# Spare weight units moved from the last expert pair to one in the middle, and one down product put off, in a three-layer fp32 transformer kernel

## The chip, the cores and the metric

One core of a Trainium2 chip runs the whole program. The metric is the device time of one execution in microseconds (us), the median over several executions. TensorE is called PE below, VectorE DVE, ScalarE ACT, GpSimd POOL, and the queue of SyncE, which issues the weight transfers, SP.

## What is computed

512 tokens of width 1024 in fp32 go through three layers. The first has differential attention, the second a pooling mixer, the third gated attention beside a linear recurrence. Each layer ends in a mixture of 32 experts of which a token uses two:

```python
def hier_moe(t, ...):                       # layers 0 and 1; layer 2 likewise with F = 256
    # group = argmax of a group router, two experts of that group by an expert router
    y[token] = sum over its 2 experts e of  w_e * (silu(t @ gate[e]) * (t @ up[e])) @ down[e]
```

gate and up are 1024 x F, down is F x 1024, with F = 512 in mixtures 0 and 1 and F = 256 in mixture 2. So a mixture reads 32 x 3 matrices of 2 MB (F = 512) or 1 MB (F = 256), once each. The result is added to the scaled input and normalized, and goes to the next layer.

## The kernel before

**Work and loops.** `mixture(l)` exists once for each engine and walks over the experts in 16 pairs (`over_pairs`, line 315; i counts turns of two pairs, q the pair in the turn, s the expert in the turn). Pair 0, 1 and 12 to 15 are written out, 2 to 11 are a hardware loop. A pair has up to 64 tokens of each of its two experts.

**PE in a pair** (line 1107): gate and up products of the first expert, then of the second (`gate_up`, line 1066); half of the rows of the next pair are gathered (`ahead`, line 970 with one-hot selection matrices, or line 1018 where mixture 2 has them gathered by DMA); the products silu(gate)*up are transposed (`turn_products`, line 1088); the other half of `ahead`; then the two down products (`down`, line 1101). In the last pair there is no next pair: `turn_last_selection` (line 1025) stands in its place, ahead of `turn_products`. ACT takes the silu of the gates (line 1385) and copies the down results out of PSUM (lines 1396, 1397), DVE multiplies (line 1844) and copies the transposed product (line 1962). POOL stores each pair's rows to `y_rows` in HBM by an indirect DMA (line 2235).

**Weights.** SP loads them in the order in which PE uses them into a ring of 12 units of 1 MB each. A matrix of 2 MB takes two units and is one transfer, unless it begins in unit 11: then it is two transfers of 1 MB (`load_matrix`, line 558). A load waits until PE has used what lay in its units 12 units earlier (`units_used`); PE counts a unit as used at the end of an expert's gates and ups, and after each half of a down matrix. A pair is 12 units with F = 512 and 6 with F = 256.

**Spares.** Places that are free in a mixture (h, hT, gaps in the work area) hold units outside the ring: 5 units in mixtures 0 and 1 (the gate and half of the up matrix of one expert, the gate of the other), 4 in mixture 2 (all gates and ups of a pair). `load_spares` issues them behind pair 0's loads, `load_scraps` (mixture 2) behind pair 1's. They belong to the last pair, experts 30 and 31, which so needs 7 (or 2) units of the ring. `gate_up_units` (line 335) and `down_unit` (line 349) give the place of each matrix in the ring's order.

**The end of a mixture.** ACT writes the scaled residual into h in the last pair (`residual`, line 1399; h is a spare until then). POOL stores pair 14, reads the number of overflow blocks and raises `over_moved` (line 2266); SP then loads tiles 0 and 1 of `y_rows` (`load_tiles`, line 631), which waits for the store of pair 14 and, in mixtures 0 and 1, for the residual. The rows of the last pair are added by PE in PSUM (`sum_last_pair`, line 672) and by DVE (`combine_tile` line 1531, `add_last` line 1557, `combine_with_last` line 1545). In mixture 2 POOL fetches the gain of the last norm (line 2244) after the store of pair 14, ahead of `over_moved`, and SP asks for all four tiles.

## Time and profile before

| | |
|---|---|
| median of 3 executions | 2067.46 us (2064.28 to 2069.76) |
| the profiled execution | 2057.91 us |
| its span, first to last instruction | 2056.1 us |
| PE / DVE / ACT / POOL busy | 1919.0 / 672.8 / 403.2 / 152.6 us |
| granted PE clock, mean | 0.983 |
| bytes moved | 598.95 MB, mean 291 GB/s |
| mixture 0, from pair 0's first product | 338.7 to 813.4 us |
| mixture 1 | 983.2 to 1455.3 us |
| mixture 2 | 1785.4 to 2032.2 us |

The profiled execution was 9.6 us shorter than the median of the three timed ones. Busy shares are averages over stages with different limits; the chain of waits, followed back from the last instruction, tells for each stretch whether PE or the weight stream set the time.

### The profile page before, as it was taken

How to read it: one execution, taken by the hardware profiler on the slowest of the kernel's cores; microseconds unless marked ns; L12 is line 12 of the kernel's file. 1: busy time of each engine (PE TensorE's matmuls, PEld its weight loads, DVE VectorE, ACT ScalarE, POOL GpSimd, SP SyncE). 2: the span in 40 equal slices, each digit the busy share in tenths (PEclk: the TensorE clock that was granted, in tenths of full speed). 3: DMA queues.
4: the chain of work that ended last, by engine and by line, in shares of the span. 5: the costliest groups of instructions: out<-in, count | busy, mean ns of one | idle time of the engine just before them, and what ended most of it. 6: DMA issues, size and time to landing. Idle time of an engine off the chain costs nothing.

```text
span 2056.1 us, 24625 instructions
## 1 busy us (share of the span) xinstructions
PE 1919.0 (93%) x9773; PEld 1036.8 (50%) x9773; DVE 672.8 (33%) x1622; ACT 403.2 (20%) x866; POOL 152.6 (7%) x208
## 2 busy tenths in 40 slices
PE   8989999999999998999999999999799999998787
PEld 4444456455545543746545545545554445765443
DVE  0156665311111112636221111111739323632114
ACT  1134431111111013110111011011324322121122
POOL 0111101000000000000100000000010001211100
PEclk9999999999999999999999999999999999999999
DMA  9711108999999996723999999998841211799995
GB/s 336 218 47 48 45 24 306 426 427 428 427 428 428 427 425 242 273 78 138 366 426 428 427 428 428 427 426 362 297 134 47 77 41 35 281 383 419 420 418 212
DMA packets 100353, 598.95 MB, mean 291 GB/s; under 512 B 14553, under 2 KB 43113, under 8 KB 61743
## 3 DMA queue, kind: packets, MB, share of 16 engines
q1 hardware_dynamic: 84639, 568.05, 68.6%
q0 software_dynamic: 15632, 29.79, 4.3%
q8 instruction: 54, 0.88, 0.2%
q14 instruction: 28, 0.23, 0.0%
HBM read 575.58 MB, written 37.03 MB: 298 GB/s over the span
## 4 chain that ended last, share of the span: by engine, by line
PE 60%; DMA 28%; DVE 7%; ACT 2%; issue 2%; SPq 1%; POOL 0%; DVEq 0%; ACTq 0%
DMA ring<-in_moe_w_up_dram 21%; PE bank L1066 19%; PE bank L713 9%; DMA ring<-in_w_up_dram 6%; PE bank L1101 6%; PE bank L866 5%; PE bank L970 5%; PE bank L727 3%; PE bank L699 3%; PE bank L1240 2%; PE bank L1201 1%; PE bank L815 1%; PE bank L1217 1%; PE bank L746 1%; DMA work<-work 1%
## 5 line engine op out<-in xcount | busy, mean ns | idle before, releaser
L1066 PE MATMUL bank<-ring,work 128*64 128x512 f32 (+1 forms) x2928 | 562.0, 532 | 53.8 <-DMA ring<-in_moe_w_up_dram 31.0
L1066 PEld LDWEIGHTS bank<-ring,work 128*64 128x64 f32 x2928 | 232.7, 140 | 370.8 <-issue 342.5
L1844 DVE TENSOR_TENSOR work<-work,bank 64x512 f32<-64x512 f32 (+1 forms) x96 | 86.4, 900 | 794.2 <-ACT work L1385 794.2
L1101 PE MATMUL bank<-ring,work 128*64 128x512 f32 x1280 | 286.9, 599 | 6.2 <-DVE work L1962 6.2
L970 PEld LDWEIGHTS bank<-work 128*128 128x128 f32 x2048 | 233.6, 192 | 25.2 <-issue 25.1
L970 PE MATMUL bank<-work 128*128 128x128 f32 x2048 | 242.7, 277 | 0.0
L713 PE MATMUL bank<-hT,ring 128*128 128x512 f32 x512 | 234.4, 599 | 0.7 <-ACT work L1303 0.7
L1101 PEld LDWEIGHTS bank<-ring,work 128*64 128x64 f32 x1280 | 90.0, 137 | 168.6 <-issue 160.7
L1385 ACT ACTIVATE work<-bank 64x512 f32<-64x512 f32 (+1 forms) x96 | 50.0, 521 | 526.1 <-PE bank L1066 525.1
L1396 ACT ACTIVATE work<-bank 64x512 f32<-64x512 f32 x96 | 56.7, 590 | 482.7 <-PE bank L1101 482.7
L713 PEld LDWEIGHTS bank<-hT,ring 128*128 128x128 f32 x512 | 92.8, 192 | 103.9 <-issue 101.9
L2235 POOL DMA_INDIRECT y_rows<-work,y_row x47 | 45.9, 977 | 984.5 <-ACT work L1397 871.4
L1836 DVE COPY work<-bank 128x512 f32<-128x512 f32 x93 | 64.3, 691 | 161.1 <-PE bank L970 154.8
L727 PE MATMUL bank<-ring,hT 128*128 128x512 f32 x192 | 83.3, 593 | 0.5 <-DMA ring<-in_attn_w_qkv_dram 0.5
L699 PE MATMUL bank<-hT,ring 128*128 128x128 f32 x512 | 61.3, 282 | 1.3 <-ACT hT L1279 1.2
L699 PEld LDWEIGHTS bank<-hT,ring 128*128 128x128 f32 x512 | 59.8, 197 | 3.2 <-ACT hT L1279 3.2
L727 PEld LDWEIGHTS bank<-ring,hT 128*128 128x128 f32 x192 | 36.2, 190 | 45.7 <-issue 44.0
L866 PE MATMUL bank<-ring,hT 128*128 128x512 f32 x128 | 57.8, 596 | 1.0 <-ACT hT L1279 1.0
L1397 ACT ACTIVATE work<-bank 64x512 f32<-64x512 f32 x96 | 57.0, 594 | 1.1
L866 PE MATMUL bank<-ring,work 128*128 128x512 f32 x128 | 56.2, 594 | 0.8 <-ACT work L1443 0.8
L1279 ACT ACTIVATE hT<-bank 128x512 f32<-128x512 f32 x56 | 31.1, 596 | 128.6 <-PE bank L746 128.5
L2179 POOL DMA_DIRECT2D work<-work x64 | 32.1, 508 | 187.9 <-ACT work L1351 187.9
(313 smaller groups left out, 1619.6 us busy)
## 6 DMA issues: line engine op xcount, KB each, us to landing
ring<-in_moe_w_down_dram SPq DMA_DIRECT2D x63, 2048.0 KB, 17.0
ring<-in_moe_w_up_dram SPq DMA_DIRECT2D x62, 2048.0 KB, 20.2
ring<-in_moe_w_gate_dram SPq DMA_DIRECT2D x60, 2048.0 KB, 16.5
ring<-in_w_down_dram SPq DMA_DIRECT2D x32, 1024.0 KB, 25.9
ring<-in_w_gate_dram SPq DMA_DIRECT2D x30, 1024.0 KB, 21.0
ring<-in_w_up_dram SPq DMA_DIRECT2D x30, 1024.0 KB, 23.0
ring<-in_attn_w_qkv_dram SPq DMA_DIRECT2D x12, 1024.0 KB, 14.2
work<-y_rows SPq DMA_DIRECT2D x12, 1024.0 KB, 7.0
```

The costliest lines, as they stand in the source:

```text
L699: mm = pe.matmul(bank[2 * i + half][:, P * tt:P * tt + P], v[:, k, P * half:P * half + P], hT[:, k, P * tt:P * tt + P], start=(k == 0), st ...
L713: mm = pe.matmul(banks[:, :], v[:, k, 128 * half:128 * half + 128], hT[:, k, :], start=(k == 0), stop=(k == K - 1))
L727: mm = pe.matmul(banks[tt][:, :], operand[:, 4 * kk + k, P * tt:P * tt + P], v[:, k, :], start=(kk + k == 0), stop=(kk + k == 4))
L866: mm = pe.matmul(bk[:, :], operand(k, tt), v[:, k % 4, :], start=(k == (0 if l else 4)), stop=(k == last))
L970: mm = pe.matmul(XT[half][:, P * k:P * k + width], src[:, tt, c0:c0 + P], sel[buf][:, tt, 0:width], start=(tt == 0), stop=(tt == T - 1))
L1066: mm = pe.matmul(GU2[of_pair][(gate_rows, up_rows)[a][of_pair], 0:F], xgT[pair % 2][:, per * kk + k, BLK * of_pair:BLK * of_pair + BLK], v ...
L1101: mm = pe.matmul(DN2[par][BLK * n:BLK * n + BLK, :], hT_[:, 2 * kk + k, BLK * par:BLK * par + BLK], v[:, k, 512 * n:512 * n + 512], start= ...
L1385: act.activation(sg_pair[own_rows[par], 0:F], GU2[par][gate_rows[par], 0:F], ACT.Silu)\
L1396: act.activation(y[own_rows[par], 0:512], DN2[par][0:BLK, :], ACT.Copy)
L1397: act.activation(y[own_rows[par], 512:D], DN2[par][BLK:P, :], ACT.Copy).then_inc(main.ysb, 1)
L1836: dve.tensor_copy(xgT[buf][:, 4 * half:4 * half + 4, 0:width], XT[half][:, :].rearrange("p (k n) -> p k n", k=4)[:, :, 0:width])\
L1844: dve.tensor_tensor(dealt(hg_pair[own_rows[par], 0:F], F // P), as_dealt(sg_pair[own_rows[par], 0:F], F // P), as_dealt(GU2[par][up_rows[p ...
```

## The change

The spares go to another pair, `SPARE_PAIR`: pair 4 in mixtures 0 and 1, pair 5 in mixture 2. From the pair behind it on every place in the ring's order is 5 (or 4) units lower, and the last pair takes all its 12 (or 6) units from the ring. In mixtures 0 and 1 the places change between even and odd, so that from there on one matrix of a pair begins in unit 11 and is loaded in two transfers. The residual moves to the pair behind the spare one. Pairs 0 to 5 are written out and 6 to 11 are the loop.

The down product of expert 29 (`put_off`), and its load, stand in the last pair behind all its gates and ups and ahead of the transposition of its products; its result is copied out, and pair 14 stored, accordingly later. `turn_last_selection` goes behind `turn_products`. The gain of the last norm is fetched one pair earlier.

```diff
+SPARE_PAIR = (4, 4, 5)
@@ over_pairs
-            for q in range(2):
-                pair(0, q)
-            with eng.Fori(1, E // TURN - 2) as i:
+            for i in range(3):
+                for q in range(2):
+                    pair(i, q)
+            with eng.Fori(3, E // TURN - 2) as i:
@@
+        def put_off(i, s):
+            return type(i) is int and TURN * i + s == E - 3
+
+        def downs(i, q):
+            own = [s for s in (2 * q, 2 * q + 1) if not put_off(i, s)]
+            return [2 * q - 1] + own if last_pair(i, q) else own
+
+        def spare_pair(m, i, q):
+            return nth_pair(i, q) == SPARE_PAIR[m.l]
+
+        def first_unit(m, i, q):
+            before = nth_pair(i, q) is not None and nth_pair(i, q) <= SPARE_PAIR[m.l]
+            return 2 * m.upb * q - (0 if before else SPARES[m.l])
+
         def gate_up_units(m, i, s):
-            first_unit, halves = 2 * m.upb * (s // 2), m.ng // 2
-            if last_pair(i, s // 2):
+            u, halves = first_unit(m, i, s // 2) - (m.nd if last_pair(i, s // 2) else 0), m.ng // 2
+            if spare_pair(m, i, s // 2):
                 if m.l == 2:
                     return {}
-                return {(1, 0): first_unit + 1, (1, 1): first_unit + 2} if s % 2 else {(1, 1): first_unit}
+                return {(1, 0): u + 1, (1, 1): u + 2} if s % 2 else {(1, 1): u}
@@ down_unit
-            return 2 * m.upb * (s // 2) + 2 * m.ng + m.nd * (s % 2) - (SPARES[m.l] if last_pair(i, s // 2) else 0)
+            if put_off(i, s):
+                return first_unit(m, i, s // 2 + 1) - m.nd + 2 * m.ng
+            spared = SPARES[m.l] if spare_pair(m, i, s // 2) else 0
+            return first_unit(m, i, s // 2) + 2 * m.ng + m.nd * (s % 2) - spared
@@ load_spares, load_scraps: the same with E - 1
-                    sp.dma_start(spare_gate[0], matrices(l, E - 2)[0]).then_inc(spare_loaded, 16)
+                    sp.dma_start(spare_gate[0], matrices(l, 2 * SPARE_PAIR[l])[0]).then_inc(spare_loaded, 16)
@@ SP, pair
-                    for s in (2 * q, 2 * q + 1):
+                    for s in downs(i, q):
@@ PE, gate_up
-                    if last_pair(i, pair) and of_pair == 0:
+                    if spare_pair(m, i, pair) and of_pair == 0:
                         pe.wait_ge(spare_loaded, spare_count[l])
@@ PE, pair
                     gate_up(i, 2 * q)
                     gate_up(i, 2 * q + 1)
+                    late, own = (downs(i, q)[:1], downs(i, q)[1:]) if last_pair(i, q) else ([], downs(i, q))
+                    for s in late:
+                        down(i, s)
+                    if not last_pair(i, q):
+                        ahead(i, q, 0)
+                    turn_products(i, q)
                     if last_pair(i, q):
                         turn_last_selection()
-                    else:
-                        ahead(i, q, 0)
-                    turn_products(i, q)
@@
-                    down(i, 2 * q)
-                    down(i, 2 * q + 1)
+                    for s in own:
+                        down(i, s)
@@ ACT, pair: also around residual(2), residual(3)
-                    if last_pair(i, q) and l < 2:
+                    if nth_pair(i, q) == SPARE_PAIR[l] + 1 and l < 2:
                         residual(0)
                         residual(1)
@@
-                    result(i, 2 * q)
-                    result(i, 2 * q + 1)
+                    for s in downs(i, q):
+                        result(i, s)
@@ POOL, mixture
-                    if l == 2 and q == E // 2 - 2:
+                    if l == 2 and q == E // 2 - 3:
                         pool.wait_ge(spare_used, 1)
                         bcast(lnp[:, D:2 * D], t["final_norm_2"].unsqueeze(0), par.rms, D)
```

## Rows read from the trace of the kernel before

**Rows 1.** The page: the chain that ended last, by line.
```profile
DMA ring<-in_moe_w_up_dram 21%; PE bank L1066 19%; PE bank L713 9%; DMA ring<-in_w_up_dram 6%; PE bank L1101 6%; PE bank L866 5%; PE bank L970 5%; PE bank L727 3%; PE bank L699 3%; PE bank L1240 2%; PE bank L1201 1%; PE bank L815 1%; PE bank L1217 1%; PE bank L746 1%; DMA work<-work 1%
```

**Rows 2.** Chain of waits, mixture 0's first pairs: start us, us, what.
```profile
338.74 13.95 PE bank L1066 x64
...
424.89 13.76 PE bank L1066 x64
...
439.45 21.00 DMA ring<-in_moe_w_up_dram
```

**Rows 3.** Chain of waits, mixture 0's pairs 14 and 15.
```profile
740.26 23.97 DMA ring<-in_moe_w_up_dram
...
764.37 8.43 PE bank L1066 x32
...
780.58 7.02 PE bank L1101 x32
...
803.11 0.67 PE bank L1088 x4
...
803.80 0.70 DVE work L1962
...
804.55 8.81 PE bank L1101 x32
...
816.76 0.70 DVE h L1557
```

**Rows 4.** Windows: us; PE, PEld, DVE, ACT, POOL busy; PEclk, DMA share, GB/s.
```profile
340.00:350.00 10.00, 10.00 (x50) 3.33 (x48) 1.63 (x3) 2.10 (x3) 2.54 (x3) 1.00 0.61 208
480.00:785.00 305.00, 288.70 (x1642) 148.16 (x1640) 47.20 (x77) 35.46 (x61) 9.73 (x10) 0.99 1.01 427
785.00:790.00 5.00, 5.00 (x26) 1.58 (x22) 0.00 (x0) 1.59 (x3) 0.39 (x1) 1.00 0.38 161
```

**Rows 5.** Chain of waits, mixture 1's pairs 14 and 15.
```profile
1409.40 7.09 PE bank L1066 x32
...
1448.23 7.11 PE bank L1101 x32
```

**Rows 6.** Chain of waits, mixture 2: pair 6, then pairs 14 and 15.
```profile
1877.34 3.69 PE bank L1066 x32
...
2010.03 3.69 PE bank L1066 x32
...
2028.49 3.68 PE bank L1101 x16
```

**Rows 7.** DMA issues, us to landing: one from 345.8 us, one from 490.1 us.
```profile
ring<-in_moe_w_gate_dram SPq DMA_DIRECT2D x1, 2048.0 KB, 8.2
...
ring<-in_moe_w_up_dram SPq DMA_DIRECT2D x1, 2048.0 KB, 21.0
```

**Rows 8.** Instructions in order of time, ACT, POOL, SP and DVE, 2014 to 2048.
```profile
2020.16 0.59 ACT L1397 ACTIVATE work<-bank 64x512 f32<-64x512 f32 x1
...
2021.53 0.97 POOL L2235 DMA_INDIRECT y_rows<-work,y_row  x1 [14.91 <-ACT work L1397]
2023.29 0.60 POOL L2160 DMA_DIRECT2D work<-in_final_norm_dram  x1 [0.79 <-PE bank L1066]
...
2026.63 2.09 SPq L639 DMA_DIRECT2D work<-y_rows  x4
...
2034.01 2.60 DVE L1531 SCALAR_TENSOR_TENSOR h<-work,h 128x1024 f32<-128x1024 f32 x2 [4.98 <-DMA work<-y_rows]
2036.65 1.41 DVE L1557 TENSOR_TENSOR h<-h,bank 128x512 f32<-128x512 f32 x2
2039.02 1.53 DVE L1545 SCALAR_TENSOR_TENSOR h<-work,bank 128x512 f32<-128x512 f32 x2 [0.97 <-PE bank L680]
```

**Rows 9.** DMA issues, us to landing: the first tile in mixture 0.
```profile
work<-y_rows SPq DMA_DIRECT2D x1, 1024.0 KB, 4.9
```

**Rows 10.** Groups of instructions: busy us, mean ns of one, idle before.
```profile
L1401 ACT ACTIVATE h<-work 128x1024 f32<-128x1024 f32 x8 | 15.5, 1996 | 0.0
```

More of the change, by code:

```diff
@@ L333, in last_pair @@
             return nth_pair(i, q) == E // 2 - 1
+        def put_off(i, s):
[8 more added lines that the diff above has]
+            return 2 * m.upb * q - (0 if before else SPARES[m.l])
         def gate_up_units(m, i, s):
-            first_unit, halves = 2 * m.upb * (s // 2), m.ng // 2
-            if last_pair(i, s // 2):
+            u, halves = first_unit(m, i, s // 2) - (m.nd if last_pair(i, s // 2) else 0), m.ng // 2
+            if spare_pair(m, i, s // 2):
                 if m.l == 2:
                     return {}
-                return {(1, 0): first_unit + 1, (1, 1): first_unit + 2} if s % 2 else {(1, 1): first_unit}
-            return {(a, kk): first_unit + m.ng * (s % 2) + halves * a + kk for a in range(2) for kk in range(halves)}
+                return {(1, 0): u + 1, (1, 1): u + 2} if s % 2 else {(1, 1): u}
+            return {(a, kk): u + m.ng * (s % 2) + halves * a + kk for a in range(2) for kk in range(halves)}
         def gu_used(m, i, s):
@@ L420, in program @@
                   con[:, C_CAUS:C_CAUS + 256], sm(128, 256)]
-        last_gates = [spare[0].rearrange("p a n -> p (a n)").rearrange("p (k n) -> p k n", k=K)[:, k, :] for k in range(K)]
-        last_ups = [spare[1].rearrange("p a n -> p (a n)").rearrange("p (k n) -> p k n", k=K)[:, k, :] for k in range(K)]
+        spare_gates = [spare[0].rearrange("p a n -> p (a n)").rearrange("p (k n) -> p k n", k=K)[:, k, :] for k in range(K)]
+        spare_ups = [spare[1].rearrange("p a n -> p (a n)").rearrange("p (k n) -> p k n", k=K)[:, k, :] for k in range(K)]
         spare_up = lnp.rearrange("p (k n) -> p k n", k=K)
@@ L531, in load_spares @@
                     sp.wait_ge(tiles_written, turns[HEADS[l][1]].src_all)
-                    sp.dma_start(spare_gate[0], matrices(l, E - 2)[0]).then_inc(spare_loaded, 16)
+                    sp.dma_start(spare_gate[0], matrices(l, 2 * SPARE_PAIR[l])[0]).then_inc(spare_loaded, 16)
                     sp.wait_ge(routing.logits, T * (l + 1))
                     for n in range(2):
-                        sp.dma_start(gaps[n], matrices(l, E - 2)[1][:, D * n:D * n + D]).then_inc(spare_loaded, 16)
-                    sp.dma_start(spare_gate[1], matrices(l, E - 1)[0]).then_inc(spare_loaded, 16)
+                        sp.dma_start(gaps[n], matrices(l, 2 * SPARE_PAIR[l])[1][:, D * n:D * n + D]).then_inc(spare_loaded, 16)
+                    sp.dma_start(spare_gate[1], matrices(l, 2 * SPARE_PAIR[l] + 1)[0]).then_inc(spare_loaded, 16)
                 def load_scraps():
@@ L541, in load_scraps @@
                     for a in range(2):
-                        sp.dma_start(spare[a].rearrange("p a n -> p (a n)"), matrices(l, E - 1)[a])\
+                        sp.dma_start(spare[a].rearrange("p a n -> p (a n)"), matrices(l, 2 * SPARE_PAIR[l] + 1)[a])\
                             .then_inc(spare_loaded, 16)
-                    gate, up, _ = matrices(l, E - 2)
+                    gate, up, _ = matrices(l, 2 * SPARE_PAIR[l])
                     sp.wait_ge(tiles_written, turns[HEADS[l][1]].src_all)
@@ L1054, in rows_of @@
                             if of_pair:
-                                return (last_gates, last_ups)[a]
+                                return (spare_gates, spare_ups)[a]
                             return [spare_up[:, k, :] for k in range(K)] if a else scraps
@@ L1410, in pair @@
                     product(i, 2 * q + 1)
-                    if last_pair(i, q) and l < 2:
+                    if nth_pair(i, q) == SPARE_PAIR[l] + 1 and l < 2:
                         residual(2)
                         residual(3)
-                    result(i, 2 * q)
-                    result(i, 2 * q + 1)
+                    for s in downs(i, q):
+                        result(i, s)
                 over_pairs(act, pair)
```

## The prediction

> **What bounds the kernel now.** I read the page first. PE is busy for 93% of the span (1919.0 of 2056.1 us), but the chain that ended last lies for 21 + 6 = 27% of it in ring transfers of the mixtures [rows 1]. So PE's busy share hides a second limit. The chain in order of time shows which holds where.
>
> In mixture 0, pairs 0 to 2 take PE (424.89 - 338.74)/3 = 28.72 us each without a wait; then a transfer ends each stretch. The last up of pair 4 lands at 439.45 + 21.00 = 460.45, that of pair 14 at 740.26 + 23.97 = 764.23 [rows 2, 3], so the stream needs 303.8/10 = 30.38 us for a pair of 12 units with its row store, 2.53 us a unit. It is never idle from 480 to 785 and then stops: share 0.38 in the next 5 us [rows 4]. PE is not done by then. From its product on pair 14's last up, at 764.37, to the end of the mixture at 804.55 + 8.81 = 813.36 it works for 49.0 us on what the ring already holds [rows 3]. **That is the place**: a late stretch set by PE while the DMA rests, after 300 us set by the DMA while PE waited. Mixture 1 is alike: 1409.40 to 1448.23 + 7.11 = 1455.34, 45.9 us [rows 5]. In mixture 2 pairs 6 to 14 take (2010.03 - 1877.34)/8 = 16.6 us, 2.76 us a unit, and PE ends at 2028.49 + 3.68 = 2032.17 [rows 6].
>
> **Spares in the middle, mixtures 0 and 1.** The stream's length stays 187 units, so the last unit can't come much earlier. What changes is what is left for PE behind it. The last needed up is now that of pair 15, with three down matrices (6 units) behind it in the order; pair 14's had 11 units behind it. So it comes 5 units later than pair 14's did: 5 x 2.53 = 12.7 us.
>
> To this comes what the stream loses where the ring is full. Pair 4 starts at 424.89 + 28.72 = 453.6 and now uses 7 units. All loads up to pair 5's last up are then landed 7 units behind 460.45: 460.45 + 17.7 = 478.2. The next, pair 5's first down matrix, may go when pair 4's first down is done. Between the products and the downs lie 28.72 - 13.76 - 7.02 = 7.94 us, so that is 453.6 + 13.76 + 7.94 + 3.51 = 478.8. A 2 MB load into a nearly empty queue took 8.2 us to land [rows 7] and so lands at 487.0, where a full queue would have had it at 478.2 + 5.1 = 483.3. I take the **loss as 3.8 us**, once; the next load that must wait goes at the end of pair 5's first gates and ups, 489.5, 2.5 us ahead of the queue's end. Bounds: 0, if the transfers still under way when a landing is told bridge the gap, and 7.6, if it runs dry twice. The Trainium skill ("DMA: Bandwidth & Descriptors", section "Anatomy of one DMA — SWDGE (gpsimd) path") has about 2 us plus the bytes at 436 GB/s for one DMA, 6.8 us for 2 MB. By it the loss would be 2.4 us, and the whole sum 2.8 us better; the row decides.
>
> **The down put off.** Behind the last up's landing PE has: gates and ups 7.1 (7.09 in mixture 1 [rows 5]), expert 29's down 3.51, transposes 0.67, then the hT copy 0.76 with the last selection's transposes beside it, two downs 7.02 [rows 3]: 19.1 us. The 3.51 us fills what is a stall today, while ACT and DVE make the last product. I let the clock stay full; 8.43 for 7.1 is the bound, as pair 14 showed [rows 3]. The down matrices land 5 us apart, ahead of their use.
>
> So the stretch is 12.7 + 3.8 + 19.1 = 35.6 us: mixture 0 gains 49.0 - 35.6 = **13.4**, mixture 1 gains 45.9 - 35.6 = **10.3**. PE alone would end mixture 0 at 453.6 + 11 x 28.72 + 13.76 + 0.67 + 0.76 + 7.02 = 791.7 (one pair's gather less), ahead of 764.4 + 35.6 = 800.0, so the stream still sets it. Its lead on PE, 12.7 - 3.8 = 8.9 us, shrinks by 30.38 - 28.72 = 1.66 us a pair: no waits in pairs 5 to 9, then waits again.
>
> **What the end of mixtures 0 and 1 gives back.** Pair 14's rows are now copied out 8.5 us before the end instead of a pair before it. ACT takes 2 x 0.59 us; in mixture 2 POOL started 0.8 us behind ACT, its store took 0.97, and SP asked 2.7 us behind POOL's last DMA, the gain's fetch (2023.89 to 2026.63) [rows 8]. The same steps stand here. So SP asks at the end - 2.8, tile 0 is there 4.9 us later [rows 9], DVE adds it in 2.60 us: end + 4.7. Today DVE goes on at 816.76, end + 3.4 [rows 3]. **Loss 1.3 us** in each, bounds 0 and 2.7. The later tiles are needed over 10 us behind the end, so their 2 us of delay are covered, as are the next layer's first loads.
>
> **Mixture 2.** Pair 15's up comes one unit later than pair 14's: 2010.03 + 2.76 = 2012.8. Then 3.69, one down at 1.84, 0.95 for half as many transposes and a smaller copy than mixture 0's 0.67 + 0.76, and 3.68: PE ends at 2023.0, 9.2 us earlier. But the tiles set the end there: DVE stood idle for them until 2034.01, and PE had been done [rows 8]. Expert 29's down ends at 2018.3, the store starts at 2020.3 instead of 2021.53 and the fetch of the gain, 1.4 us with its wait, is out of the way: SP asks at 2024.0 instead of 2026.63. The first tile took 2034.01 - 2026.63 = 7.4 us behind that fetch, 4.9 in mixture 0 [rows 8, 9]; I take 4.9, the nearer case now. DVE then has tile 0 done at 2024.0 + 4.9 + 2.60 + 1.41 = 2032.9 instead of 2039.02: **gain 6.1**, with 7.4 it is 3.6. The stream there runs no risk of a full ring: 4 units of lead in a ring that holds two pairs.
>
> **At nothing:** the residual (four copies of 2.0 us on ACT, two and two, in pair 5 [rows 10]) lies under 6.9 us of PE products and 7.9 us of gathers; without that cover it would hold up pair 5 once, by 4 us. The two half transfers per pair cost SP one more issue, under loads queued 21 us ahead [rows 7]. The spares are landed long before pair 4: the DMA ran empty in 340 to 350 [rows 4]. More code written out: pairs 12 to 15 are so today under a full stream and show no other wait.
>
> **Sum:** 13.4 + 10.3 + 6.1 - 2 x 1.3 = 27.2 us. The profiled execution, 2057.91, would be 2030.7; it was 9.6 us under the median of 2067.46, against which I forecast **2040.3 us**.
>
> **Rivals.**
> - *The stream loses nothing* and the tiles cover their delay: 2 x (3.8 + 1.3) = 10.2 us more, 2030.1. For it: the share of 1.01 through every earlier wait. Chance 0.22.
> - *The ends take more back*: the queue runs dry twice in each (7.6 more), and each end loses 2.7 (2.8 more): 2050.7. With the slow clock and the late tile too, 2.6 + 2.5, 2055.8. For it: every step of the ask is on the path now. Chance 0.21.
> - *The change moves the lead but doesn't use it*: the ring can't hold the 5 units' lead, the stream rests 12.7 us in pairs 4 and 5 and ends that much later. Then 2 x 8.9 = 17.8 us and mixture 2's 6.1 fall away: 2064.2. Against it: at 453.6 about 21 us of loads are under way, more than 12.7 [rows 7]. Chance 0.04.
> - *Slower: the ring's edge.* Behind the spare pair the places are odd, a matrix straddles the edge, and SP holds everything behind its half. If the queue ran dry once in every pair from 5 on, at 8.2 - 5.1 = 3.1 us each, 11 of them would cost 34.1 in place of 3.8, in both mixtures 60.6 us more: 2100.9. It turns slower from 27.2/(2 x 3.1), 4 to 5 more dry spells in each mixture. Against it: loads lay 21.0 us in the queue, four matrices. Chance 0.03.
>
> **How the numbers follow.** The forecast has 0.50. The range from the best to the worst sum, 2028 to 2056, takes in the first two rivals and 2 us of spread of the medians. A measurement can tell about 0.3% (6.2 us) from no change; the first three cases, forecast included, are faster by more: 0.93. The fourth is the same: 0.04. Slower: 0.03.
>
> **What would show it.** Right: no PE wait for a ring transfer in pairs 5 to 9 of mixtures 0 and 1, small ones from 10 on; a dip of the DMA near 479; pair 15's last up landing near 780.5, mixture 0 ending 35 to 36 us behind pair 14's old landing, at 800; DVE waiting for tile 0 at each end; mixture 2's SP request before the down products' end plus 2 us. Wrong: a DMA share under 0.9 over more than 5 us in the middle, a wait on `spare_loaded`, or a half unit ending a PE wait in every pair.

## The result and the profile after

| | before | after |
|---|---|---|
| median of 4 executions each | 2068.61 us (2064.28 to 2070.09) | 2040.17 us (2039.23 to 2048.76) |
| ratio | | 0.9875, 95% interval 0.9844 to 0.9906 |
| the profiled execution / its span | 2057.91 / 2056.1 us | 2040.23 / 2038.4 us |
| PE busy | 1919.0 us | 1915.2 us |

The medians differ by 28.4 us; the ratio, with which the interval goes, says 1.25%, 26 us. The change is faster. The forecast was 2040.3 us and 27.2 us of gain.

The two profiled executions differ by only 17.7 us, and that must be cleared up before they are compared. In the changed one, mixture 0 starts at 348.25, in the other at 338.74 [rows 2]. That is 9.5 us in a part that the change does not touch; over the thirteen profiles of this study this start lay between 338.7 and 348.8. So I cut every profiled execution into stages that begin and end with a product of PE. "mixture" is its first gate product to the end of its last down product, "between" from there to the next mixture's first product, "end" from mixture 2's last down product to the end of the span, "waits" what PE stood idle for ring transfers in mixtures 0 and 1.

| us | to mixture 0 | mixture 0 (waits) | between | mixture 1 (waits) | between | mixture 2 | end |
|---|---|---|---|---|---|---|---|
| before | 338.7 | 474.6 (16.6) | 169.9 | 472.1 (14.4) | 330.0 | 246.8 | 24.0 |
| after | 348.2 | 460.6 (6.7) | 172.5 | 463.5 (9.8) | 328.0 | 239.4 | 26.1 |

The mixtures give 14.0 + 8.6 + 7.4 = 30.0 us. The stretch behind each takes some back: the next layer's projection starts 12.9 us behind mixture 0's last down instead of 10.7, 19.0 behind mixture 1's instead of 17.4, and the end is 2.1 longer: 5.9 us. That makes **24.1 us**. The other 3.1 us, with which span and start would give 27.2, lie in untouched work between the mixtures, nearly all between 1 and 2, where the profiles scatter too (327.6 to 333.4).

The page's chain by line. The transfers of the ring were 21 + 6% [rows 1] and are 12 + 5%:

```profile
PE bank L1091 22%; DMA ring<-in_moe_w_up_dram 12%; PE bank L738 9%; PE bank L1126 8%; PE bank L995 8%; PE bank L891 5%; DMA ring<-in_w_up_dram 5%; PE bank L724 3%; PE bank L752 3%; PE bank L1268 1%; PE bank L1229 1%; PE bank L840 1%; DMA work<-work 1%; PE bank L1245 1%; PE bank L771 1%
```

The chain of waits in mixture 0 of the changed kernel (start us, us, what). L1091 are gates and ups (L1066 before), L1126 downs (L1101), L1424 ACT's first copy of a down result, L1585 the first tile's sum with the last pair's rows, L724 the next layer:

```profile
463.24 13.73 PE bank L1091 x64
...
577.36 13.76 PE bank L1091 x64
...
591.85 21.07 DMA ring<-in_moe_w_up_dram
...
711.08 23.28 DMA ring<-in_moe_w_up_dram
...
734.50 8.78 PE bank L1091 x32
...
758.08 13.73 PE bank L1091 x64
...
779.59 3.58 PE bank L1126 x16
783.17 13.83 PE bank L1091 x64
797.00 3.45 PE bank L1126 x16
...
800.47 0.59 ACT work L1424
...
802.44 3.89 DMA y_rows<-work,y_row
...
806.39 5.01 DMA work<-y_rows
...
814.07 0.70 DVE h L1585
...
821.92 8.01 PE bank L724 x64
```

Read it against [rows 2, 3]. Pair 4, which has the spares now, starts at 463.24, and pairs 4 to 8 follow each other without a wait. The first wait is in pair 9, begun 28.5 us behind pair 8, at 605.9: its last up lands at 591.85 + 21.07 = 612.92. The last is in pair 13. **Pairs 14 and 15 don't wait at all**: their 64 gate and up products run in one piece (13.73 and 13.83). Behind the last up that it needed from the stream PE had 49.0 us of work before; now this is pair 15's last up, and from its product (783.17 + 6.87 = 790.04) to the end are 808.90 - 790.04 = 18.9 us. The trace has no landing for that up; the second down matrix behind it landed at 799.58, and at 4.9 us a matrix (the landing of the last one, 804.47, less 799.58) I estimate 789.8 for the up. So PE waits for nothing from 734.50 on, but at the end the stream is only some 0.3 us ahead of it.

PE at the end of mixtures 0 and 2, in order of time (start us, us, engine, line, operation, tiles; in brackets the idle time before):

```profile
800.37 0.66 PE L1113 MATMUL bank<-con,work 128*128 128x128 f32 x4
800.86 0.60 PE L1050 MATMUL bank<-con,work 128*128 128x128 f32 x4
801.81 7.09 PE L1126 MATMUL bank<-ring,work 128*64 128x512 f32 x32 [0.35 <-DVE work L1990]
...
2008.67 3.65 PE L1126 MATMUL bank<-ring,work 128*64 128x512 f32 x16
```

The turned selection (L1050) lies ahead of the copy for which PE waits anyway; 0.35 us of idle time are left before the last downs.

The windows show what the forecast called the dip (us; PE, PEld, DVE, ACT, POOL busy; granted PE clock, DMA share, GB/s). It was put near 479 and lies at 485 to 490, which is 9.5 us later, like everything:

```profile
480.00:485.00 5.00, 5.00 (x45) 4.76 (x45) 1.50 (x3) 0.00 (x0) 0.00 (x0) 1.00 1.00 426
485.00:490.00 5.00, 5.00 (x26) 1.70 (x24) 0.48 (x1) 1.18 (x2) 0.00 (x0) 1.00 0.48 144
490.00:495.00 5.00, 5.00 (x26) 1.61 (x24) 0.00 (x0) 1.18 (x2) 0.97 (x1) 1.00 0.91 383
600.00:700.00 100.00, 97.02 (x544) 47.98 (x542) 13.98 (x21) 13.00 (x22) 3.88 (x4) 1.00 1.01 427
```

Against 427 GB/s the two middle windows lack (427 - 144)/427 x 5 = 3.3 and 0.5 us, their two neighbours behind some tenths: the stream **ran dry for about 4.3 us**, 4.2 in mixture 1. In all other 5 us windows of the middle it is full.

The end of mixture 2: the chain, then DVE in order of time:

```profile
2002.39 3.67 PE bank L1091 x32
...
2009.78 2.65 DMA y_rows<-work,y_row
...
2012.50 4.70 DMA work<-y_rows
```

```profile
2017.23 2.60 DVE L1559 SCALAR_TENSOR_TENSOR h<-work,h 128x1024 f32<-128x1024 f32 x2 [7.91 <-DMA work<-y_rows]
```

SP asks 0.2 us behind PE's last down (2008.67 + 3.65 = 2012.32), DVE stands idle for 7.91 us, and the chain goes through the store and the first tile: the tiles set the end now. In the kernel before they did not. DVE was idle for them too, 4.98 us [rows 8], but waited once more behind them, 0.97 us for PE's sum of the last pair [rows 8], and the chain of before goes through that sum:

```profile
2038.06 0.87 PE bank L680 x2
...
2039.02 0.76 DVE h L1545
```

e1 and e10 below agree: their first tile is there 3.7 us earlier, counted from PE's last down, and their end is as long as before (23.9 in both, 24.0 before).

### The profile page after: what moved, and what is told of

Read it like the earlier page. It is cut to its first block, busy times and chain, and to the rows that moved or that the text cites. A ratio compares the mean times of both kernels' runs of the same rounds, so it can differ in the third digit from the quotient of the medians.

```text
span 2038.4 us, 24272 instructions
## 1 busy us (share of the span) xinstructions
PE 1915.2 (94%) x9773; PEld 1032.6 (51%) x9773; DVE 673.2 (33%) x1622; ACT 402.3 (20%) x866; POOL 152.3 (7%) x208
## 4 chain that ended last, share of the span: by engine, by line
PE 68%; DMA 20%; DVE 7%; ACT 2%; issue 2%; SPq 0%; POOL 0%; another core or an unknown queue 0%; DVEq 0%; POOLq 0%
PE bank L1091 22%; DMA ring<-in_moe_w_up_dram 12%; PE bank L738 9%; PE bank L1126 8%; PE bank L995 8%; PE bank L891 5%; DMA ring<-in_w_up_dram 5%; PE bank L724 3%; PE bank L752 3%; PE bank L1268 1%; PE bank L1229 1%; PE bank L840 1%; DMA work<-work 1%; PE bank L1245 1%; PE bank L771 1%
## 5 line engine op out<-in xcount | busy, mean ns | idle before, releaser
L1091 PE MATMUL bank<-ring,work 128*64 128x512 f32 (+1 forms) x2928 | 555.8, 528 | 36.3 <-DMA ring<-in_w_up_dram 18.8
L1091 PEld LDWEIGHTS bank<-ring,work 128*64 128x64 f32 x2928 | 227.3, 138 | 352.8 <-issue 326.2
L1126 PE MATMUL bank<-ring,work 128*64 128x512 f32 x1280 | 285.8, 596 | 4.2 <-DVE work L1990 4.1
L1126 PEld LDWEIGHTS bank<-ring,work 128*64 128x64 f32 x1280 | 89.2, 137 | 165.2 <-issue 156.9
L1424 ACT ACTIVATE work<-bank 64x512 f32<-64x512 f32 x96 | 56.6, 589 | 475.4 <-PE bank L1126 475.4
L724 PE MATMUL bank<-hT,ring 128*128 128x128 f32 x512 | 60.6, 280 | 1.5 <-ACT hT L1307 1.5
L724 PEld LDWEIGHTS bank<-hT,ring 128*128 128x128 f32 x512 | 59.1, 195 | 3.4 <-ACT hT L1307 3.4
L1307 ACT ACTIVATE hT<-bank 128x512 f32<-128x512 f32 x56 | 30.9, 595 | 127.7 <-PE bank L771 127.7
## 6 DMA issues: line engine op xcount, KB each, us to landing
ring<-in_moe_w_up_dram SPq DMA_DIRECT2D x61, 2048.0 KB, 16.6
```

What stands on the lines that cost most here:

```text
L724: mm = pe.matmul(bank[2 * i + half][:, P * tt:P * tt + P], v[:, k, P * half:P * half + P], hT[:, k, P * tt:P * tt + P], start=(k == 0), st ...
L1091: mm = pe.matmul(GU2[of_pair][(gate_rows, up_rows)[a][of_pair], 0:F], xgT[pair % 2][:, per * kk + k, BLK * of_pair:BLK * of_pair + BLK], v ...
L1126: mm = pe.matmul(DN2[par][BLK * n:BLK * n + BLK, :], hT_[:, 2 * kk + k, BLK * par:BLK * par + BLK], v[:, k, 512 * n:512 * n + 512], start= ...
L1424: act.activation(y[own_rows[par], 0:512], DN2[par][0:BLK, :], ACT.Copy)
```

## The experiments

Eleven runs were made in three groups, each group on a chip of its own with the kernel before beside it: e1 to e4 (before: 2065.06 us), e5 to e8 (2060.25) and e9 to e11 (2063.27). Each had 5 or 6 executions, e2 twelve. None leaves work out. A median compares only within its group. Stages as above, in us, from one profiled execution each; "behind 0" and "behind 1" are the start of the next projection behind the mixture's last down.

| | median | ratio to before, 95% | mixture 0 | behind 0 | mixture 1 | behind 1 | mixture 2 | end |
|---|---|---|---|---|---|---|---|---|
| before | | | 474.6 | 10.7 | 472.1 | 17.4 | 246.8 | 24.0 |
| after | 2040.17 | 0.9875, 0.9844 to 0.9906 | 460.6 | 12.9 | 463.5 | 19.0 | 239.4 | 26.1 |
| changed again (e11) | 2041.07 | 0.9892, 0.9875 to 0.9908 | 460.9 | 12.7 | 461.7 | 18.6 | 238.4 | 26.2 |
| e1 spares only | 2046.25 | 0.9914, 0.9896 to 0.9931 | 464.5 | 10.7 | 465.4 | 17.4 | 240.8 | 23.9 |
| e2 down put off only | 2067.29 | 1.0006, 0.9990 to 1.0021 | 470.2 | 12.9 | 472.1 | 21.2 | 245.5 | 26.7 |
| e3 gain fetched late | 2043.36 | 0.9893, 0.9875 to 0.9911 | 460.8 | 12.5 | 463.8 | 18.7 | 237.4 | 27.6 |
| e4 spares at pair 2 | 2050.96 | 0.9930, 0.9911 to 0.9950 | 465.2 | 12.3 | 469.1 | 18.9 | 238.4 | 26.1 |
| e5 spares at pair 6 | 2032.23 | 0.9874, 0.9850 to 0.9898 | 461.0 | 12.0 | 459.7 | 18.8 | 239.6 | 26.2 |
| e6 eight pairs written out | 2039.89 | 0.9908, 0.9886 to 0.9930 | 461.5 | 12.4 | 461.6 | 18.7 | 237.8 | 26.2 |
| e7 four spares | 2036.57 | 0.9883, 0.9860 to 0.9905 | 460.3 | 14.3 | 464.7 | 19.0 | 238.2 | 26.2 |
| e8 spares at pair 12 | 2040.35 | 0.9903, 0.9880 to 0.9926 | 466.4 | 11.9 | 465.8 | 18.9 | 238.0 | 26.6 |
| e9 spares in two pairs | 2038.48 | 0.9880, 0.9863 to 0.9898 | 458.8 | 12.7 | 459.8 | 19.0 | 238.6 | 27.6 |
| e10 as e9, no put-off in 2 | 2040.82 | 0.9890, 0.9871 to 0.9909 | 461.9 | 12.5 | 459.1 | 19.8 | 241.4 | 23.9 |

The stages leave out the untouched stretches, which scatter by 10 us, but they scatter too. Profiles of the same order of work differ by 3.1 us in mixture 0 (e9, e10), by 2.2 in mixture 1 (after, e3, e6, e11) and by 2.2 in mixture 2 (237.4 to 239.6 in the nine with the changed order). What is smaller than that is not shown by one profile, and where the executions say something else than the stages, it is said.

### e1, e2: each part alone

```diff
 # e1: nothing is put off (the places in the ring follow, here and in e2)
-            return type(i) is int and TURN * i + s == E - 3
+            return False
-            return [2 * q - 1] + own if last_pair(i, q) else own
+            return own
 # e2: the spares stay in the last pair, the residual with them; six pairs written out, gain fetched early
-SPARE_PAIR = (4, 4, 5)
+SPARE_PAIR = (15, 15, 15)
```

> The spares sit in the middle, expert 29's down stays in pair 14. Theory (the stream sets the end, and the put-off gives only what lies behind the last landing): pair 15's last up lands 2 units (5.1 us) later, behind it PE has 17.3 instead of 19.1 us, so each of mixtures 0 and 1 is 3.3 us longer than in the changed kernel (460.7 and 463.6 us from first product to last down), and the end of a mixture gets back the 1.3 to 2.7 us that the late store of pair 14 costs. Mixture 2 is 1 to 2 us longer and its end shorter by as much. In all 0 to 4 us above the changed kernel: 2040 to 2044 us. Rival (the put-off down is what gains, because it fills the stall behind the last products in all three mixtures and keeps the clock up): 10 us or more above the changed kernel.

> The spares stay in the last pair, only the down is put off (and the last norm's gain is fetched before the store of pair 14). Theory: PE's late stretch behind pair 14's last up shrinks by the stall of some 3 us in mixtures 0 and 1, the end of each gives 1.3 to 2.7 us back, so 0 to 4 us under the kernel before. Rival (the put-off carries the gain): 10 to 20 us under the kernel before.

With the spares alone the mixtures are 10.1 + 6.7 + 6.0 = 22.8 us shorter than before, and nothing comes back behind them (10.7, 17.4, 23.9). Its six executions say less: 0.86%, 17.8 us, interval 14 to 21; the profiled one was the fastest of them, 7.6 us under their median, which at 2046.25 lies above the 2040 to 2044 expected. The chain of e1 shows why the ends stay as they were: pair 14's rows are stored in time, SP asks 13.5 us ahead of mixture 0's end (804.95), and DVE goes on from PE's products alone.

```profile
764.55 22.88 DMA ring<-in_moe_w_up_dram
...
787.57 7.10 PE bank L1091 x32
...
797.84 7.11 PE bank L1126 x32
...
808.35 0.70 DVE h L1585
```

SP's queue in e1, in order of time:

```profile
791.42 1.49 SPq L664 DMA_DIRECT2D work<-y_rows  x2
```

Against e1, putting the down off shortens the mixtures by 3.9, 1.9 and 1.4 us, 7.2 together, and lengthens what is behind them by 2.2, 1.6 and 2.2, 6.0 together: 1.2 us of gain. With e11 in place of the first profile it is 9.7 and 5.5, 4.2 us, and e3, which differs from the changed kernel by the gain's fetch alone, has a median 2.9 us under e1's. All of this is inside the scatter. Alone (e2) the put-off is no gain: where 0 to 4 us were expected, the ratio is 1.0006 and the stages give 5.7 us in the mixtures and lose 8.7 behind them. So **the spares carry the change**; the put-off down is worth 1 to 4 us there, less than can be told. It fills one stall and opens another: pair 14's rows, needed by all that follows, come a pair later. e1 also has the residual and the last selection moved, the early fetch and six pairs written out; e3 and e6 test the last two, the first two were not run apart.

### e3: the gain fetched where it was

```diff
-                    if l == 2 and q == E // 2 - 3:
+                    if l == 2 and q == E // 2 - 2:
```

> The changed kernel with the last norm's gain fetched behind the store of pair 14 again. Theory: SP asks for the tiles of mixture 2 about 1.4 us later and the first tile lands up to 2.5 us later behind the fetch's traffic: 1.4 to 3.9 us above the changed kernel, all of it behind mixture 2's last down. Rival (the request hangs on the store's landing, not on POOL's next steps): under 0.5 us.

The end is 27.6 us, 1.5 longer. SP asks at 2009.70, 0.2 us behind PE's last down as in the changed kernel, so the fetch doesn't hold up the request; that hangs on the landing of pair 14's store. The first tile is there 6.2 us behind the request in place of 4.7: in this trace the late fetch costs only as a neighbour of the tiles. The ratio can't show it, and the end scatters by as much: e9 fetches early and has 27.6 too, since its store took 3.87 us to land and not 2.65.

### e4, e5, e6, e8: where the spares go

```diff
-SPARE_PAIR = (4, 4, 5)
+SPARE_PAIR = (2, 2, 5)     # e5: (6, 6, 5); e8: (12, 12, 5), with twelve pairs written out
@@ e5, and e6 with the old SPARE_PAIR: two more pairs written out
-            for i in range(3):
+            for i in range(4):
-            with eng.Fori(3, E // TURN - 2) as i:
+            with eng.Fori(4, E // TURN - 2) as i:
```

> Spares of mixtures 0 and 1 at pair 2 instead of 4. Theory (the ring is full when the spare pair comes, and the stream runs dry for the time that it was ahead): at pair 2 the stream is about 3.3 us further ahead of PE, so its dry time is 7.1 instead of 3.8 us and each of mixtures 0 and 1 is 3.3 us longer, 464 and 467 us; 6.6 us in all, 2047 us. Rival (the ring's odd places, not the full ring, make the stream dry): no change in mixtures 0 and 1 beyond 1 us.

> Spares of mixtures 0 and 1 at pair 6, eight pairs written out and four in the loop. Theory: by pair 6 the stream is no longer ahead, so the spare pair leaves no dry time in it (no window under 0.9 there), and PE is late for 3.7 us in pairs 4 and 5 instead; the end comes 3 us earlier in each of mixtures 0 and 1 than in the changed kernel (458 and 460 us, where the clock stays full at the end), 4 to 7 us in all: 2034 to 2036 us. Rival (PE's work from the first wait on already sets the end, so nothing is left in the stream): 0 to 2 us, since PE's start of pair 6 is later by as much as the stream gains.

> The changed kernel with eight pairs written out instead of six, nothing else moved: the control for the run with the spares at pair 6. Theory: instructions come in time, no difference within 1 us in any mixture. Rival (written-out code has to be fetched through a full DMA queue): each mixture longer by some us, with PE idle for no transfer.

> Spares of mixtures 0 and 1 at pair 12, twelve pairs written out. Theory: PE waits for the stream up to pair 11 as in the kernel before, and from pair 12 on its own work sets the end: 3.9 us later than in the changed kernel in each of mixtures 0 and 1, 8 us in all, 2048 us. Rival (the place does not matter as long as it is not the last pair, since the stream's length sets the end): within 1 us of the changed kernel.

**e4** is the test of the full ring. Two pairs earlier, the stream leads PE by 3.3 us more (two pairs of 30.38 - 28.72), and the surplus must be lost. The windows of e4 (columns as above):

```profile
420.00:425.00 5.00, 5.00 (x44) 4.72 (x43) 1.90 (x3) 0.59 (x1) 0.00 (x0) 1.00 0.93 338
425.00:430.00 5.00, 5.00 (x39) 3.71 (x39) 1.14 (x2) 0.00 (x0) 0.00 (x0) 1.00 0.40 167
430.00:435.00 5.00, 5.00 (x26) 1.60 (x24) 0.00 (x0) 1.19 (x2) 0.00 (x0) 1.00 0.45 134
```

The three windows of e4 lack 7.5 us together, 3.2 more than in the changed kernel, and mixture 0 is 4.6, mixture 1 5.6 us longer. The executions agree: the median is 7.6 us over e3's, where 6.6 in all were expected. A stream rest in the middle is paid at the end; that the stages lost 1.4 and 2.4 us more than the 3.2 is about their scatter.

**e5** was to have no dry time at pair 6, and has 3.2 us of it. Its windows:

```profile
535.00:540.00 5.00, 5.00 (x39) 3.90 (x40) 1.47 (x3) 0.00 (x0) 0.00 (x0) 1.00 0.95 400
540.00:545.00 5.00, 5.00 (x26) 1.70 (x24) 0.00 (x0) 1.19 (x2) 0.00 (x0) 1.00 0.55 177
```

I had taken the lead that the stream still has at pair 4 for its cause, but at pair 6 that lead is about nothing. What remains is the step of five units at once, and I work it out so: the spare pair uses 7 units of the ring, and these land within 7 x 2.53 = 17.7 us, while PE frees the next place only 6.9 + 7.9 + 3.5 = 18.3 us behind its middle, and that load is a lone one and needs 7.6 us to land (issued at 488.38 in the changed kernel), where a full queue lands a matrix every 5.1: 18.3 + 7.6 - 17.7 - 5.1 = 3.1 us of dry time. e7 and e9, which take smaller steps, bear it out; e8 shows that it isn't all.

The mixtures of e5 are 0.5 and 1.9 us shorter than those of its control e6, which is within the scatter. Its executions are better than that: the median is 7.7 us under e6's, four of its six lie under the fastest of e6. That is what was expected (2034 to 2036), by a mechanism that the trace denies, and the two profiles don't show where it comes from. So pair 6 may be the better place; why stays open.

**e6**: no mixture is more than 0.9 us longer than in the changed kernel: more code written out costs nothing that can be seen, as forecast.

**e8**: at pair 12 the spares come when PE has waited for the stream in the pairs before, and from pair 12 on PE sets the end alone. The chain of e8, pairs 11 to 15:

```profile
652.16 24.52 DMA ring<-in_moe_w_up_dram
...
676.81 8.58 PE bank L1088 x32
...
700.19 13.73 PE bank L1088 x64
...
728.72 13.73 PE bank L1088 x64
...
782.35 13.73 PE bank L1088 x64
```

Four pairs without a wait: the lead that the spares give is not used up when the mixture ends. Mixtures 0 and 1 are 4.9 and 4.2 us longer than e6's, where 3.9 stood: 2.9 and 2.6 us more of waits, part of the rest at the slow clock (mixture 0 has two products of 8.78 and 8.58 us, e6's one). But the executions don't bear it out: medians of 2040.35 and 2039.89 us, where 8 us more were expected. The stream runs dry here too, and for longer:

```profile
720.00:725.00 5.00, 5.00 (x32) 2.71 (x32) 0.69 (x1) 0.00 (x0) 0.00 (x0) 1.00 0.21 88
725.00:730.00 5.00, 5.00 (x26) 1.72 (x24) 0.00 (x0) 2.37 (x4) 0.00 (x0) 1.00 0.79 279
```

These lack 4.0 + 1.7 us, at a place where the stream has no lead at all and five units alone would make it 3.1. A slow product just before it (8.58 for 7.1 us) makes PE free its places 1.5 us later and would be part of it; no run settles the rest. So an early place (pair 2) loses by stages and executions, the last pair by both, and between pairs 4, 6 and 12 the stages and the executions don't give one order.

### e7: one spare unit less

```diff
-SPARES = (5, 5, 4)
+SPARES = (4, 4, 4)
@@ gate_up_units: both halves of expert 8's up come through the ring
-                return {(1, 0): u + 1, (1, 1): u + 2} if s % 2 else {(1, 1): u}
+                return {(1, 0): u + 2, (1, 1): u + 3} if s % 2 else {(1, 0): u, (1, 1): u + 1}
```

> Four spare units instead of five in mixtures 0 and 1: in mixture 0 all places stay even, so that no matrix straddles the ring's edge; in mixture 1 every place is odd from pair 0 on. Theory (a unit outside the ring is worth one unit's time, and the edge costs nothing): both mixtures 0 and 1 are 2.5 us longer than in the changed kernel, less up to 1 us of dry time, 3 to 5 us in all: 2043 to 2045 us. Rival (the straddling matrix costs): mixture 0 as fast as before or faster than in the changed kernel, mixture 1 slower by well over 2.5 us.

I had counted 2.5 us a unit. Mixture 0 is 0.3 us shorter, mixture 1 1.2 longer, and the median lies 3.3 us under e6's, so the unit is not missed. The window at the dip says what went against it; the dip is nearly gone:

```profile
485.00:490.00 5.00, 5.00 (x26) 1.62 (x24) 0.00 (x0) 2.37 (x4) 0.00 (x0) 1.00 0.87 315
```

That lacks 1.3 us. Summed over the same 35 us around the dip, e7 lacks 2.0 us in mixture 0 and 2.4 in mixture 1, the changed kernel by this count 4.2 and 4.4. **The fifth spare of one pair should buy 2.5 us and costs 2.1 of dry time.** Mixture 0 has no split transfer here; in mixture 1, which begins at an odd place, nearly every pair has a split up matrix (28 transfers of 1 MB of up matrices against none in mixture 0). Against e6 on the same chip mixture 0 is 1.2 us shorter and mixture 1 3.1 us longer. That is the sign that a cost of the splits would have, at the edge of the scatter, so e7 doesn't settle whether they are free.

### e9, e10, e11: the five spares in two pairs

```diff
+SECOND = 6
@@ eight pairs written out as in e6; first_unit and down_unit follow the two steps
@@ gate_up_units: pair 4 takes gate 8 and half of up 8 from spares, pair 6 the gate of expert 13
-                return {(1, 0): u + 1, (1, 1): u + 2} if s % 2 else {(1, 1): u}
+                return {(0, 0): u + 1, (0, 1): u + 2, (1, 0): u + 3, (1, 1): u + 4} if s % 2 else {(1, 1): u}
+            if nth_pair(i, s // 2) == SECOND and m.l < 2 and s % 2:
+                return {(1, 0): u + 4, (1, 1): u + 5}
@@ load_spares
-                    sp.dma_start(spare_gate[1], matrices(l, 2 * SPARE_PAIR[l] + 1)[0]).then_inc(spare_loaded, 16)
+                    sp.dma_start(spare_gate[1], matrices(l, 2 * SECOND + 1)[0]).then_inc(spare_loaded, 16)
 # e10, beside this: no put-off in mixture 2
-            return type(i) is int and TURN * i + s == E - 3
+            return l < 2 and type(i) is int and TURN * i + s == E - 3
```

> In mixtures 0 and 1 three of the five spare units are used in pair 4 and two in pair 6, instead of all five in pair 4; eight pairs are written out instead of six, as in the control e6; mixture 2 is as changed. Theory of the full ring: with all five in pair 4 the stream ran dry for 4.3 us (mixture 0) and 4.2 us (mixture 1). With three of them the free room of the ring is never far enough behind for the queue to empty, and the two of pair 6 come when PE's lead is small again. So no 5 us window in the middle has a DMA share under 0.9, the stream ends 3.7 to 4.3 us earlier in each mixture, mixture 0 takes 457, mixture 1 459 to 460, and the whole is 7 to 8 us under the changed kernel on the same chip: about 0.9835 to 0.985 of the kernel before. Rival, the late products set the end and not the dry spell: mixtures 0 and 1 gain 2 us together at most, the ratio is that of the changed kernel within 0.001. Against the theory speaks the run with four spares, where 3.0 us less dry time paid only for the unit given away.

> As e9, and in mixture 2 the 30th expert's down stands where it stood before the change. From the run with the spares alone, the put-off was worth 1.4 us in mixture 2 and cost 2.2 us at its end: so mixture 2 takes 240.8 and the end 23.9, together 0.8 us less than e9, which is under what five rounds can tell; only the stages can show it. Rival: the put-off in mixture 2 pays (the end stays at 26 although nothing is put off): 1.4 us more than e9.

> The changed kernel once more, as the comparison on the same chip for the two above: mixture 0 460.6 and mixture 1 463.5, each within 1.7 us (one product at the slow clock), ends 12.9, 19.0 and 26.1, ratio to the kernel before 0.9875 to 0.991.

In e9 the dry spell is gone. The windows behind pair 4's and pair 6's use of the spares:

```profile
480.00:490.00 10.00, 10.00 (x55) 4.15 (x55) 0.69 (x1) 2.37 (x4) 0.00 (x0) 1.00 1.00 423
...
540.00:545.00 5.00, 5.00 (x26) 1.72 (x24) 0.00 (x0) 1.19 (x2) 0.00 (x0) 1.00 0.95 380
```

But mixtures 0 and 1 are only 2.1 and 1.9 us shorter than in e11, about half of what was expected, and in e10, the same work there, 1.0 longer and 2.6 shorter. The medians on the same chip are 2038.48 and 2041.07 us, 2.6 us apart where 7 to 8 were expected; e10's is 2040.82. e11 itself came out as expected but for mixture 1, 1.8 us shorter. The chain in mixture 0 shows for this pair of profiles where the other half is. e9, pairs 13 and 14:

```profile
728.66 7.10 PE bank L1098 x32
...
736.22 23.17 DMA ring<-in_moe_w_up_dram
...
759.52 7.09 PE bank L1098 x32
```

e11, pairs 13 and 14:

```profile
708.86 23.63 DMA ring<-in_moe_w_up_dram
...
732.62 8.65 PE bank L1091 x32
...
756.07 13.73 PE bank L1091 x64
```

Mixture 0 began at 344.8 in e9, at 345.9 in e11. PE begins pair 13's last half 728.66 - 344.8 = 383.9 us behind the start in e9, 732.62 - 345.9 = 386.7 in e11: the stream is 2.8 us earlier. In e11 this was the last wait and PE sets the rest; in e9 the stream still sets pair 14, 759.52 - 728.66 = 30.9 us on, where PE alone takes 28.5. That gives 2.3 us back, and of the rest 1.55 us is only the clock (8.65 against 7.10 us): 2.8 - 2.3 + 1.55 = 2.1. So the dry spell is real, and what its removal brings the stream is lost again where PE is the limit; in this pair of profiles 0.5 us is left beside the clock. Of all versions only e5 lies clearly under its control, in its executions and not in its stages.

In mixture 2, e10 is 2.8 us longer than e9 (241.4 against 238.6) and its end 3.7 shorter (23.9 against 27.6). The difference, 0.9 us, is what was expected, but 1.4 of the 3.7 are the late store of e9; against the changed kernel's 26.2 (e11) e10 gets 2.3. The medians (2040.82 against 2038.48) go the other way. What e10 shows is that the end goes back to its old length when nothing is put off.

## Why the prediction was right

The time came out at 2040.17 where 2040.3 stood, closer than the forecast's terms deserve. One by one:

| step | forecast | measured |
|---|---|---|
| mixture 0 shorter | 13.4 | 14.0 |
| mixture 1 shorter | 10.3 | 8.6 |
| mixture 2, PE's end earlier | 9.2 | 7.4 |
| behind mixtures 0 and 1, longer | 1.3 and 1.3 | 2.2 and 1.6 |
| behind mixture 2, longer | 9.2 - 6.1 = 3.1 | 2.1 |
| sum | 27.2 | 24.1 |

- **The place was right.** What bounded mixtures 0 and 1 was a late stretch of 49 us that PE worked alone behind 300 us in which it waited. e1 shows that moving the spares alone gives 22.8 us by its stages and 17.8 by its executions, and e2 that without it there is no gain.
- **The dry time of the stream was right in size and place**: 4.3 and 4.2 us for 3.8 (bounds 0 and 7.6). e4 makes it longer and pays for it, e7 and e9 make it shorter. With the landing time of the trace, 8.2 us [rows 7], the forecast had 3.8; the Trainium skill ("DMA: Bandwidth & Descriptors", section "Anatomy of one DMA — SWDGE (gpsimd) path"), whose fit is for DMAs that GpSimd issues while SyncE issues these, gave an estimate of 2.4. The lone load took 7.6 us here, between the two (6.8 and 8.2) and a little nearer to the row of the trace.
- **The waits came back in pair 9**, one pair earlier than forecast, and by 0.3 us only: the lead was 12.7 - 4.3 = 8.4 us and not 8.9, and shrinks by 1.85 a pair and not by 1.66, since PE takes (577.36 - 463.24)/4 = 28.53 us for a pair here. 8.4 - 5 x 1.85 is below nothing.
- **Mixture 0: 14.0 for 13.4.** The stretch from the spare pair's start to the end came as forecast: 799.4 in the old count (808.90 - 9.51) for 800.0. The forecast had the stream set the end, and small waits up to it; in the trace the last wait is in pair 13, and then PE and the stream reach that last up together, the stream an estimated 0.3 us ahead. That mixture 0 gains more than mixture 1 is in the forecast only because two products at the end of the one trace of before ran at the slow clock there (8.43 and 8.81 us for 7.1 [rows 3]), 3.1 us, and none in mixture 1 [rows 5]. The stall ahead of the second of them is in e1 too, and there it took 7.11. So 3.1 of the 13.4 us were the luck of one profile, and the changed kernel's mixture 0 has a slow product of its own (8.78).
- **Mixture 1: 8.6 for 10.3, a term that was mis-sized.** "I let the clock stay full" was the step. After its last wait, in pair 14, the product ran for 8.78 us and not 7.1 (8.43 stood beside it as the bound); that is 1.7 us, the whole gap. From there on PE set the end here, not the stream. The same happened in mixture 0, in pair 13, and is in its 14.0. The chain in mixture 1:

```profile
1399.16 8.78 PE bank L1091 x32
```

- **Mixture 2: 7.4 for 9.2.** Behind the last up PE took 9.9 us (2002.39 to 2012.32), forecast 10.2: right. The last up itself came 229.5 us behind the mixture's start (1772.9); pair 14's had come 224.6 behind it, and one unit of 2.76 was allowed for where it took 4.9. Why the stream lost 2.1 us there no run settles; the other eight profiles with this order have 237.4 to 239.6 in the stage, 238.3 in the mean, so half of it is scatter.
- **The ends: 2.2, 1.6 and 2.1.** The mis-sized step in mixtures 0 and 1 is that "SP asks at the end - 2.8, tile 0 is there 4.9 us later". SP asks 2.5 us ahead of mixture 0's end and the tile is there 5.0 us later, so that DVE comes to the last pair's rows at 814.07, 5.2 us behind the end and not 4.7; 0.4 us more come in behind it. SP's request hangs on the landing of the store, 3.89, 2.83 and 2.65 us on the chain, which the forecast took as a distance from POOL's last DMA. The value stayed inside its bounds (0 and 2.7). In mixture 2 the forecast said that "the tiles set the end there" before the change; they did not, PE's sum did, and putting the down off is what brought the tiles onto the path, for 2.1 us. The number held since the forecast compared with 2039.02, which stands behind PE's sum.
- **The gain fetched early**: of its two terms the one on the tile's landing shows in e3 (4.7 us against 6.2, where 4.9 and 7.4 stood), the one on the request, "1.4 us with its wait, is out of the way", does not: SP asks at the same moment in both.
- Of the rivals, "the lead moved but not used" falls with e1 and the chain. "Slower, the ring's edge" falls with the windows of the changed kernel, where no dry spell repeats in the pairs behind (427 GB/s from 600 to 700); a small cost of the edge is not excluded (e7). "The stream loses nothing" falls with the windows. "The ends take more back" was partly true: the ends of mixtures 0 and 1 lost 1.2 us more than forecast, of the 2.8 that it had for them, and the slow clock came in once in each of these mixtures, 1.7 us each.

That the sum of 27.2 and the median agree within 0.2 us is luck: the stages give 24.1, and the interval of the ratio holds 19 to 32 us. The changed kernel run again gave 22.3 (1.08% of 2063.27, interval 19 to 26). Both intervals hold the stages' 24.1.

## What to carry to other kernels

Look in the chain for the last wait of a stage, and then at what the other engine still has to do behind it: prefetched work in store is worth more in the middle, where the stream sets the time, than at the end, where it doesn't. Release it in steps no larger than what the consumer frees while the stream refills, or the ring runs full and the queue empties: here the fifth unit at once bought nothing that could be measured. Before an operation is put off to fill a stall, follow its result: the put-off down saved 7.2 us on PE and cost 6.0 in the tiles behind it. An engine that stands idle for a transfer is not yet bound by it: see what it waits for next. And set the profile of one execution beside the times of the others; twice here they disagreed by more than the effect looked for.

## What was not expected of the hardware

- After the longer waits of PE the granted clock fell for a moment. The windows of the changed kernel behind the wait of 2.22 us in pair 13 (columns as above):

```profile
732.00:734.40 2.40, 0.28 (x2) 0.00 (x0) 1.45 (x3) 0.59 (x1) 0.00 (x0) 1.00 0.99 418
734.50:736.00 1.50, 1.50 (x4) 0.50 (x6) 0.06 (x1) 0.00 (x0) 0.00 (x0) 0.55 0.99 421
736.00:738.00 2.00, 2.00 (x8) 0.79 (x6) 0.00 (x0) 0.00 (x0) 0.00 (x0) 0.50 1.04 440
738.00:740.00 2.00, 2.00 (x12) 0.79 (x10) 0.00 (x0) 0.00 (x0) 0.00 (x0) 0.99 0.99 422
```

  The granted clock is at 0.50, the lower of its two levels (1.2 of 2.4 GHz), for some 3.3 us, which costs 1.7 us. In all thirteen traces there are 165 products of 32 matmuls behind a wait for an up in mixtures 0 and 1. The 126 behind 0.2 to 1.94 us of idle time took 7.1 us, the 12 behind 2.47 to 3.32 us took 8.4 to 8.8, and of the 27 between 1.95 and 2.38 us 13 were slow. So one wait of 2.5 us costs 4.2, two of 1.25 cost 2.5, and this is a part of the scatter between equal kernels. Not only such waits do it: the last downs of mixture 0 in the kernel before took 8.81 us, at a granted clock of 0.50 from 805 to 808, behind idle pieces of 1.19 and 0.78 us, while in e1, behind 1.74 and 0.35 us, they took 7.11.
- An indirect store of 64 rows whose landing is waited for took 3.89, 2.83 and 2.65 us at the ends of mixtures 0, 1 and 2, in mixture 0 with the stream's last matrix still under way (landed at 804.47, the store was issued at 802.44), and 10 to 11 us under a full stream (issued at 760 and 727 in mixture 0).
- The start of mixture 0 lay between 338.7 and 348.8 us in the thirteen profiles without any change to the work before it, and with it every later time of the trace moves. Single profiled spans are for that reason no measure of a gain of this size; stages from product to product are a better one, to about 3 us a mixture.
